# The FFN norms of a two-block network: weight and 1/rms applied behind the transposition of x

## The reference

```python
def rms_norm(x, g):
    y = x * lax.rsqrt(jnp.mean(x * x, axis=-1, keepdims=True) + 1e-6)
    return y * g
def swiglu(x, w_in, w_out):
    a, b = jnp.split(x @ w_in, 2, axis=-1)
    return (jax.nn.silu(a) * b) @ w_out
# block 1
x = x + 0.5 * swiglu(rms_norm(x, ffn1_norm), ffn1_w_in, ffn1_w_out)
u = rms_norm(x, mix_norm) @ w_in      # then RG-LRU, block and memory attention -> mixed
x = x + mixed @ w_out
x = x + 0.5 * swiglu(rms_norm(x, ffn2_norm), ffn2_w_in, ffn2_w_out)
# block 2
for l in range(2):
    h = rms_norm(x, ffn1_norm_pre[l])
    x = x + 0.5 * rms_norm(swiglu(h, ffn1_w_in[l], ffn1_w_out[l]), ffn1_norm_post[l])
    h = rms_norm(x, mix_norm_pre[l])
    x = x + rms_norm(token_mixer(h, mem, ...), mix_norm_post[l])
    h = rms_norm(x, ffn2_norm_pre[l])
    x = x + 0.5 * rms_norm(swiglu(h, ffn2_w_in[l], ffn2_w_out[l]), ffn2_norm_post[l])
```

## Time and profile before

| | us |
|---|---|
| median of 3 runs | 1834.89 (1832.85 to 1840.52) |
| the profiled execution | 1835.6 |
| its span | 1833.6 |
| busy: TensorE | 1795.9 (98%) |
| busy: VectorE | 1059.6 (58%) |
| busy: ScalarE | 910.9 (50%) |
| busy: GpSimd | 45.3 (2%) |

### The profile page before, as it was taken

How to read it: one execution, slowest core, us unless ns; L and a number is a source line. 1 busy time by engine, 2 the same in 40 slices (tenths; PEclk the granted TensorE clock), 3 DMA queues, 4 the chain that set the end, 5 groups by cost and what they waited for, 6 DMA issues and landing times.

```text
span 1833.6 us, 33276 instructions
## 1 busy us (share of the span) xinstructions
PE 1795.9 (98%) x13114; PEld 1658.6 (90%) x13114; DVE 1059.6 (58%) x1393; ACT 910.9 (50%) x1180; POOL 45.3 (2%) x66
## 2 busy tenths in 40 slices
PE   8999998999999999999999999999999999999998
PEld 8999877999999999888899999899999888989997
DVE  5545776554565456565676544554564657675454
ACT  5344565444453445566655344444454566644443
POOL 0000220000000000000000000000000000000000
PEclk9999999999999999999999999999999999999999
DMA  8555423655575555443354554555545442445552
GB/s 313 204 186 202 173 95 113 214 199 185 178 250 185 186 181 207 174 170 116 119 204 168 188 186 176 209 206 190 198 161 211 173 169 94 161 150 207 190 197 94
DMA packets 47857, 329.19 MB, mean 180 GB/s; under 512 B 5393, under 2 KB 5649, under 8 KB 9617
## 3 DMA queue, kind: packets, MB, share of 16 engines
q1 hardware_dynamic: 44496, 316.84, 48.0%
q10 hardware_dynamic: 3264, 11.03, 1.9%
HBM read 326.80 MB, written 1.05 MB: 179 GB/s over the span
## 4 chain that ended last, share of the span: by engine, by line
issue 82%; PE 14%; ACT 2%; POOL 1%; DVE 1%; DMA 0%; DVEq 0%; POOLq 0%; ACTq 0%
PE work L1494 3%; PE work L1493 3%; PE work L1495 3%; PE acc L1493 1%; PE acc L1495 1%; PE acc L1494 1%; POOL rstd L552 1%; ACT prob L720 0%; PE work L1576 0%; PE acc L1586 0%; PE work L1552 0%; DMA const<-const 0%; PE acc L1712 0%; ACT squared L621 0%; ACT hi L609 0%
## 5 line engine op out<-in xcount | busy, mean ns | idle before, releaser
L1003 DVE TENSOR_TENSOR lo<-raw,hi 128x2048 fp32r<-128x2048 f32 x280 | 640.0, 2291 | 468.0 <-ACT hi L601 467.8
L1493 PE MATMUL work<-xT_hi,hi 128*128 128x256 f32 x2752 | 768.4, 279 | 6.9 <-DVE lo L1003 6.4
L1495 PE MATMUL work<-xT_hi,lo 128*128 128x256 f32 x2752 | 763.8, 278 | 0.0
L1494 PE MATMUL work<-xT_lo,hi 128*128 128x256 f32 x2752 | 763.8, 278 | 0.0
L601 ACT ACTIVATE hi<-raw 128x2048 fp32r<-128x2048 f32 x280 | 533.9, 1910 | 236.0 <-PE work L1495 190.3
L1493 PEld LDWEIGHTS work<-xT_hi,hi 128*128 128x128 f32 x2752 | 518.4, 188 | 17.4 <-DVE lo L1003 8.2
L1494 PEld LDWEIGHTS work<-xT_lo,hi 128*128 128x128 f32 x2752 | 518.7, 188 | 2.5
L1495 PEld LDWEIGHTS work<-xT_hi,lo 128*128 128x128 f32 x2752 | 519.4, 189 | 0.0
L1495 PE MATMUL acc<-hi,hT_lo 128*128 128x512 f32 x480 | 189.1, 394 | 0.0
L1494 PE MATMUL acc<-lo,hT_hi 128*128 128x512 f32 x480 | 188.2, 392 | 0.0
L1493 PE MATMUL acc<-hi,hT_hi 128*128 128x512 f32 x480 | 186.9, 389 | 0.0
(11 more groups left out here) (262 smaller groups left out, 1950.7 us busy)
## 6 DMA issues: line engine op xcount, KB each, us to landing
raw<-stream SPq DMA_DIRECT2D x298, 1024.0 KB, 4.8
pre<-pre ACTq DMA_DIRECT2D x7, 512.0 KB, 5.4
mem_in<-mem ACTq DMA_DIRECT2D x3, 1024.0 KB, 7.1
post<-post ACTq DMA_DIRECT2D x6, 512.0 KB, 3.7
x<-x SPq DMA_DIRECT2D x2, 512.0 KB, 4.9
pre<-pre SPq DMA_DIRECT2D x2, 512.0 KB, 3.7
out<-x SPq DMA_DIRECT2D x4, 256.0 KB, 2.0
alibi<-alibi ACTq DMA_DIRECT2D x1, 768.0 KB, 14.8
```

What stands on the lines that cost most here:

```text
L1003: nc.vector.tensor_tensor(lo[:, s, :], raw[:, s, :], hi[:, s, :].bitcast(F32), ALU.subtract).then_inc(lo_ready, 1)
L1493: nc.tensor.matmul(dst, a_hi, b_hi, start=start, stop=False)
L1494: nc.tensor.matmul(dst, a_hi, b_lo, start=False, stop=False)
L1495: return nc.tensor.matmul(dst, a_lo, b_hi, start=False, stop=stop)
```

## The change

- For k = 0 and 3 TensorE transposes x as it is (`x_turned`, 16 transposes of 128 x 128), half by half as x comes, with no sum of squares awaited. The norm's weight is a scale per channel at the evacuation (`x_gain` in `x_high` and `x_low`). Its 24 columns come with the parameters; `pre` and its loads are gone.
- 1/rms comes later. The squares stand behind `x_high`; VectorE spreads 1/rms over a tile (`norm_spread`), TensorE turns it into a row between the first chunk's low products, ScalarE writes it out (`row_out`). A new pass on VectorE, `scaled_a`, multiplies a by it, in every chunk, and the silu works in place on the result. For b the factor is put into the residual: `half_rstd` in block 1; in a layer the post-norm divides it out and only its epsilon is scaled (`norm_eps`).
- `first_chunk` does the high products of the first two units together, except in the first FFN.
- For k = 2 VectorE scales the rows of x by 1/rms (`x_scaled`, 128 x 1024), and 16 transposes follow when both tiles are ready.
- The split of the second unit behind an FFN is taken out of `ffn` and comes behind the norm chain (`B1_MEM + 1`, `L_MEM + 1`), for the second FFNs behind the last post sums.
- Parameters have a semaphore of their own (`params_loaded`), the ring is continuous (`slot`), the loads on SyncE are ordered anew, and the layers are written out in Python on all engines.

The diff, cut to its core and moved left by eight columns ("..." and the hunk lines mark what is left out):

```diff
@@ -491,12 +496,13 @@
...
+def turned_bank(k, r):
+    return acc[:, r, :] if k == 2 else (work[:, 2, :], work[:, 3, :], acc[:, 0, :], acc[:, 1, :])[r]
+def x_gain(sec, k):
+    return (b1p if sec.layer is None else lp)("g_x")[:, KD * (k - k // 2):KD * (k - k // 2) + KD]
@@ -507,32 +513,34 @@
...
+    load(0)
+    sp.dma_start(params[:, KD * 3:B1P_N], b1_params[:, KD * 3:B1P_N]).then_inc(params_loaded, 16)
+    load(1)
+    load(2)
+    at = RING
+    for layer in range(LAYERS):
+        base = B1_UNITS + layer * L_UNITS
+        turns = (base + 1 - at) // RING
+        load_turns(at, at + RING * turns)
+        at += RING * turns
+        sp.dma_start(params[:, 0:LP_N], l_params[layer]).then_inc(params_loaded, 16)
+    turns = (UNITS - at) // RING
+    load_turns(at, at + RING * turns)
+    for n in range(at + RING * turns, UNITS):
+        load(n)
@@ -595,44 +602,48 @@
...
     def x_squares(sec, r, i):
         for c in range(2):
-            act.wait_ge(x_ready, sec.at(12, 12, 4 * r + 2 * i + c + 1))
-            x_half_squares(i, c)
+            if sec.layer is None and r == -1:
+                act.wait_ge(x_loaded[i], 16)
+            else:
+                act.wait_ge(x_ready, sec.at(12, 12, 4 * r + 2 * i + c + 1))
+            nc.scalar.activation(xs[:, i, cols(c)], x[:, i, cols(c)], ACT.Square,
+                                 accum_out=sums[:, 2 * i + c:2 * i + c + 1]).then_inc(sq_ready, 1)
...
     def x_high(sec, k):
...
+        gain = x_gain(sec, k)
+        for r in range(4):
+            act.wait_ge(xT_ready, sec.at(16, 16, 4 * k + r + 1))
+            for c in range(2):
+                kt = 2 * r + c
+                ins = nc.scalar.activation(xT_hi[:, kt, :], turned_bank(k, r)[:, T * c:T * c + T], ACT.Copy,
+                                           scale=gain[:, kt:kt + 1])
+            ins.then_inc(xhi_ready, 1)
+    def row_out(sec, k):
+        act.wait_ge(spread_turned, sec.at(*ROWS, k + 1))
+        nc.scalar.activation(norm_row, work[:, 2, 0:T], ACT.Copy, scale=ROOT_D).then_inc(row_ready, 1)
@@ -647,11 +658,10 @@
...
+        def silu(j):
+            act.wait_ge(scaled_ready, c0 + j + 1)
+            nc.scalar.activation(silu_a, silu_a, ACT.Silu).then_inc(silu_ready, 1)
@@ -661,21 +671,22 @@
...
         split_high(sec, u0 + 2)
-        silu(0, u0)
+        row_out(sec, k)
         split_high(sec, u0 + 3)
+        silu(0)
...
         with act.Fori(1, CHUNKS - 1) as j:
-            silu(j, u0 - 1, j)
             split_high(sec, u0 + 2, j)
+            silu(j)
             split_high(sec, u0 + 3, j)
             high_h(j, u0 + 1, j)
@@ -686,8 +697,6 @@
...
-        if more:
-            split_high(sec, u0 + FFN_UNITS + 1)
@@ -734,22 +743,19 @@
...
     act.wait_ge(half_set, 2)
     nc.scalar.activation(trig[:, 0, 0, :], neg_half[:, 0:ROT], ACT.Square)
+    act.wait_ge(params_loaded, 32)
+    x_high(sec, 0)
+    split_high(sec, B1_FFN1)
+    split_high(sec, B1_FFN1 + 1)
     for i in range(TT):
-        act.wait_ge(x_loaded[i], 16)
-        for c in range(2):
-            x_half_squares(i, c)
-    split_high(sec, B1_FFN1)
-    x_high(sec, 0)
-    split_high(sec, B1_FFN1 + 1)
-    load_pre(sec, 1)
+        x_squares(sec, -1, i)
@@ -759,10 +765,10 @@
     ffn(sec, B1_FFN1, 0, lambda: mem_squares(sec), b1p("g_mem"))
     for i in range(TT):
         x_squares(sec, 0, i)
+    split_high(sec, B1_MEM + 1)
     split_high(sec, B1_MEM + 2)
+    x_high(sec, 2)
     split_high(sec, B1_MEM + 3)
-    x_high(sec, 2)
@@ -830,36 +836,34 @@
...
-    split_high(sec, B1_OUT + 4)
+    split_high(sec, B1_FFN2)
+    split_high(sec, B1_FFN2 + 1)
+    x_high(sec, 3)
     for i in range(TT):
         x_squares(sec, 1, i)
-    x_high(sec, 3)
-    split_high(sec, B1_FFN2 + 1)
...
+    ffn(sec, B1_FFN2, 1, angles)
+    split_high(sec, B1_UNITS + 1)
...
+    for layer in range(LAYERS):
         sec = Section(layer)
...
+        act.wait_ge(params_loaded, 16 * (3 + layer))
+        x_high(sec, 0)
+        load_post(sec, 0)
         for i in range(TT):
             x_squares(sec, -1, i)
-        split_high(sec, L_FFN1)
-        x_high(sec, 0)
...
             post_sums(sec, 0, L_MEM - 1, i)
             x_squares(sec, 0, i)
+        split_high(sec, L_MEM + 1)
@@ -984,13 +987,16 @@
             split_high(sec, L_OUT + w + 2)
         for i in range(TT):
             post_sums(sec, 1, L_FFN2 - 1, i)
+        split_high(sec, L_FFN2 + 1)
+        x_high(sec, 3)
+        load_post(sec, 2)
+        for i in range(TT):
             x_squares(sec, 1, i)
-        load_post(sec, 2)
-        x_high(sec, 3)
-        split_high(sec, L_FFN2 + 1)
-        ffn(sec, L_FFN2, 1, more=False)
+        ffn(sec, L_FFN2, 1, more=layer + 1 < LAYERS)
         for i in range(TT):
             post_sums(sec, 2, L_UNITS - 1, i)
+        if layer + 1 < LAYERS:
+            split_high(sec, L_UNITS + 1)
@@ -1013,39 +1019,42 @@
...
+    def x_scaled(sec, p, i):
+        dve.wait_ge(x_ready, sec.at(12, 12, 2 * i + 2))
+        dve.wait_ge(sq_ready, sec.at(14, 14, 6 + 2 * i + 2))
+        ask_root(i, sums[:, 2 * i:2 * i + 2], D * EPS)
         root_ready(sec, p)
-        nc.vector.tensor_scalar(diag[:, i, :], ident, rstd[:, i:i + 1], ROOT_D, ALU.mult, ALU.mult).then_inc(xs_ready, 1)
+        nc.vector.tensor_scalar(xs[:, i, :], x[:, i, :], rstd[:, i:i + 1], ROOT_D, ALU.mult, ALU.mult).then_inc(xs_ready, 1)
+    def norm_spread(sec, k, p):
+        dve.wait_ge(sq_ready, sec.at(14, 14, (4, 14)[k]))
+        parts = sums[:, 0:2 * TT].rearrange("p (i c) -> p i c", c=2)
+        nc.vector.scalar_tensor_tensor(var[:, 0:TT], parts[:, :, 0], D * EPS, parts[:, :, 1], ALU.add, ALU.add).then_inc(pow_asked, 1)
+        root_ready(sec, p)
+        nc.vector.tensor_copy(spread, rstd[:, 0:TT].unsqueeze(2).to_broadcast([P, TT, P])).then_inc(spread_ready, 1)
+        if sec.layer is None:
+            return step.mark(nc.vector.tensor_scalar(half_rstd, rstd[:, 0:TT], 0.5 * ROOT_D, None, ALU.mult))
+        return step.mark(nc.vector.tensor_scalar(norm_eps, var[:, 0:TT], EPS, None, ALU.mult))
     def x_low(sec, k):
...
+        for r in range(4):
+            dve.wait_ge(xhi_ready, sec.at(16, 16, 4 * k + r + 1))
+            for c in range(2):
+                kt = 2 * r + c
+                ins = nc.vector.scalar_tensor_tensor(xT_lo[:, kt, :], turned_bank(k, r)[:, T * c:T * c + T], gain[:, kt:kt + 1],
+                                                     xT_hi[:, kt, :].bitcast(F32), ALU.mult, ALU.subtract)
+            ins.then_inc(xlo_ready, 1)
     def mem_scaled(sec, p):
@@ -1066,6 +1075,13 @@
...
+        def scaled_a(j, n, trip=0):
+            dve.wait_ge(unit_used, sec.unit(n + 1) + trip * RING)
+            wait(dve, h_ready, c0 + j)
+            nc.vector.tensor_tensor(silu_a.rearrange("p (c t) -> p c t", c=2), work[:, 0, :].rearrange("p (c t) -> p c t", c=2),
+                                    norm_row.unsqueeze(1).to_broadcast([P, 2, T]), ALU.mult).then_inc(scaled_ready, 1)
         def gated(j, n, trip=0):
@@ -1079,6 +1095,8 @@
...
         split_low(sec, u0 + 2)
+        dve.wait_ge(row_ready, sec.at(*ROWS, k + 1))
+        scaled_a(0, u0)
         split_low(sec, u0 + 3)
@@ -1086,12 +1104,14 @@
...
         with dve.Fori(1, CHUNKS - 1) as j:
+            scaled_a(j, u0 - 1, j)
@@ -1103,23 +1123,21 @@
...
-            nc.vector.scalar_tensor_tensor(x[:, i, cols(c)], acc[:, 2 * i + c, :], scale, x[:, i, cols(c)], ALU.mult,
+            nc.vector.scalar_tensor_tensor(x[:, i, cols(c)], acc[:, 2 * i + c, :], scale or half_rstd[:, i:i + 1], x[:, i, cols(c)], ALU.mult,
                                            ALU.add).then_inc(x_ready, 1)
...
         for c in range(2):
             dve.wait_ge(ysq_ready, sec.at(0, 12, 4 * r + 2 * i + c + 1))
             if c == 1:
-                ask_root(2 + i, ysums[:, 2 * i:2 * i + 2])
+                ask_root(2 + i, ysums[:, 2 * i:2 * i + 2], eps)
@@ -1161,16 +1179,14 @@
...
-    dve.sem_inc(lo_ready, 1)
-    dve.wait_ge(ident_loaded, 16)
-    for i in range(TT):
-        x_scaled(sec, 0, i, i)
+    dve.wait_ge(params_loaded, 32)
     x_low(sec, 0)
     split_low(sec, B1_FFN1)
     split_low(sec, B1_FFN1 + 1)
+    step.after(norm_spread(sec, 0, 0))
@@ -1178,11 +1194,12 @@
...
+        residual(sec, 0, B1_MEM - 1, i, None)
+        x_scaled(sec, 2 + i, i)
+    split_low(sec, B1_MEM + 1)
     split_low(sec, B1_MEM + 2)
+    x_low(sec, 2)
     split_low(sec, B1_MEM + 3)
-    x_low(sec, 2)
@@ -1284,12 +1301,12 @@
...
+    split_low(sec, B1_FFN2)
     for i in range(TT):
         residual(sec, 1, B1_FFN2 - 1, i, 1.0)
-        x_scaled(sec, 3, 8 + i, i)
     x_low(sec, 3)
     split_low(sec, B1_FFN2 + 1)
+    step.after(norm_spread(sec, 1, 7))
@@ -1309,29 +1326,25 @@
...
+    for layer in range(LAYERS):
...
+        dve.wait_ge(params_loaded, 16 * (3 + layer))
         x_low(sec, 0)
-        split_low(sec, L_FFN1)
         split_low(sec, L_FFN1 + 1)
...
+        step.after(norm_spread(sec, 0, 0))
```

(60 more changed lines are left out.)

286 lines of the change are left out of this document (93 added, 193 removed).

## The result

The changed kernel takes 1847.94 us (median of 6 runs, 1847.03 to 1848.42), the kernel before 1833.21 us beside it (6 runs). The ratio is 1.0062, with a 95% interval of 1.0039 to 1.0085: slower by 0.6%, where 1817.8 us and a gain were forecast. The profiled execution has a span of 1846.3 us, 12.7 more than before.

What follows compares the result with a forecast made beforehand. TensorE was taken as busy nearly the whole span. Entries 23.8 plus block 1's mix norm 3.3, less layers' mix norms 7.6 and start 2.4, give 17.1 us off: median 1834.89 to 1817.8, range 1806 to 1827.

Steps and rivals of the forecast that it cites:

- What stays: Inside an FFN: a chunk stays 16 us of TensorE without a gap; the added VectorE pass and moved silu cost nothing.
- signs that the prediction gave for being wrong: No mix-norm wait, TensorE waiting for `silu_a` or `scaled_a`, or engine pauses in the straight code where the loop was.
- Rival C: Chunk loop: `scaled_a` holds bank 0 so TensorE stands 0.4 us in each of 66 chunks; 1844 us, chance 0.03.
- entry of layer 0: First FFN of layer 0: fillers, fp32 passes and waiting go, first chunk ends at 509.3 instead of 514.4; gain 5.1 us.
- entry of layer 1: First FFN of layer 1: no back-edge pause, first chunk ends at 1174.5 instead of 1183.5; gain 9.0 us, the largest term.
- block 1 mix norm: Mix norm in block 1: squares start earlier because the second unit's split moves behind the norm; gain 3.3 us.
- entry of block 1's FFN2: Second FFN of block 1: first chunk ends at 323.6 instead of 326.4; gain 2.8 us.
- layers' mix norm: Mix norm in each layer: the late split of `L_MEM + 1` stalls TensorE 4.3 us and lowers its clock; loss 3.8 us.
- entries of the layers' FFN2: Second FFN in each layer: first chunk ends at 985.2 instead of 988.65; gain 3.4 us, twice.
- start: Kernel start: evacuating x waits for all parameters, then the first split; first product at 16.0; loss 2.4 us (0 to 4).
- Rival B: FFN entries: the norm row comes late (6 us) or the clock drops (3 to 6 us); about 1823 us, chance 0.25.
- Layers written out: Layer loops as straight code: waits lose register arithmetic, taken as nothing; bounded by 2.4 us gain or loss a layer.

Runs made afterwards that it cites:

- good layout: The changed kernel with 160 unused bytes a partition behind the parameters: 1813.9 us, ratio 0.9873 to the kernel before.
- the run with the other start: The good layout with the first unit split before x is evacuated, fillers mostly behind the transposes, and alibi and mem_in loaded later: 1807.3 us.

## Why the prediction was wrong, point by point

**The step that failed** is the first sentence of "What stays": that a chunk keeps its time because its instructions and waits stay. The step of a TensorE product depends on where the buffers lie, and the change moved them by 96 bytes and by 4000: the in step went from 113.6 to 116.7 ns and the chunk from 16.40 to 16.80 us. Against the good layout the span is 31.8 us longer (1846.3 and 1814.5), 22.8 of it in the bodies and the rest nearly all in the stages between. No rival named it, and of the signs that the prediction gave for being wrong none came: they are waits and pauses, and this loss shows in neither. The length of a chunk was misread besides: the earlier trace rows show a window of 16 us that 119 products touch, and the chunk lasts 16.40. Rival C had the right price, 0.4 us a chunk and 1844, for a mechanism that is not there: no wait for `scaled_a`, and the pass done twice costs nothing. It would have been right for a wrong reason.

On the good layout (`room(160)`), whose steps and chunks are those of the kernel before, the span is 19.0 us shorter; 17.1 were forecast. By its terms:

| term | forecast | measured on the good layout |
|---|---|---|
| entry of layer 0 | 5.1 | 4.7 |
| entry of layer 1 | 9.0 | 8.6, of it 3.3 by the layers written out alone |
| block 1 mix norm | 3.3 | 3.5 (10.86 to 7.39) |
| entry of block 1's FFN2 | 2.8 | 2.9 (the rest of that stage's 6.4) |
| layers' mix norm | -3.8 each | -2.9 each (15.06 to 17.95) |
| entries of the layers' FFN2, and all else in their mix stages | 3.4 each | 5.5 and 3.9 |
| start | -2.4 | -4.6 |

The sum is nearer than its terms: misses of about 2 us, the start one way and the layers' stages the other, cancel in part. That is luck.

**The entries** were read well. In the changed kernel's timeline of layer 0's entry, whose last product starts at 502.33, against the earlier trace rows:

```profile
502.56 0.60 PE L1614 MATMUL work<-const,x 128*128 128x128 f32 x4
...
503.91 0.84 ACT L639 ACTIVATE xT_hi<-work,params 128x256 fp32r<-128x256 f32 x2 [2.03 <-PE work L1614]
...
504.89 0.47 PE L1560 MATMUL work<-xT_hi,hi 128*128 128x256 f32 x2 [0.42 <-ACT xT_hi L639]
```

Products start 2.3 us after the end of the last one; 2.2 were forecast, 0.4 of it a wait for pair 0. **Rival B's clock drop** did not come: the granted clock of the stretch with the transposes and of the one behind it is 1.00.

```profile
502.50:504.90 2.40, 1.98 (x18) 1.71 (x16) 0.80 (x2) 0.99 (x3) 0.00 (x0) 1.00 0.73 299
504.90:508.00 3.10, 3.10 (x26) 3.10 (x27) 3.10 (x9) 3.10 (x10) 0.00 (x0) 1.00 0.50 169
```

It was 1.00 at the entries of block 1's FFN2 and of the layers' FFN2, too. The Trainium skill, "TensorE: Matmul & The Clock Gate", Part 4: PE-mode transpose, says that transpose mode does not count as being busy for the clock. The prediction took drops as likely by that; with 1.98 us of transposes in these 2.40 us none came, and these runs do not test a longer stretch of them.

**The mix norm** had the right mechanism. The stall was 3.0 us (4.3 forecast), the clock fell as said, and the edit that puts the split early takes both away. The price of a drop was right, too: 1.6 us forecast, and 1.6 to 1.7 between the layer norms of the good layout with one drop (17.9, 18.0 us) and the one without in the run with the other start (16.3). What the prediction did not have is that the drop can stay away.

**The start** had the right order and one thing missed: the fillers. They stood in TensorE's queue ahead of the transposes and held them, although x had landed at 6.3 us and the parameters at 10.8 (11.0 forecast). Until 10.3 us they start 0.21 us apart and from then on 0.11. The clock column reads 1.00 for both stretches, so that the first one ran at the lower level is inferred from the spacing alone.

```profile
5.19 6.25 PE L1605 MATMUL work<-const 128*128 128x128 f32 x32 [5.19 <-DMA const<-const]
...
11.27 0.60 PE L1614 MATMUL work<-const,x 128*128 128x128 f32 x4
...
17.51 1.86 PE L1560 MATMUL work<-xT_hi,hi 128*128 128x256 f32 x7 [4.33 <-ACT hi L608]
```

The first product came at 17.5, not 16.0, and 26 products took the next 4.5 us at a granted clock of 0.67, where I had put 1.6 us for the clock in all. In the good layout's run the clock there was 0.50 for 5.9 us, from the first product on.

```profile
17.50:22.00 4.50, 4.49 (x26) 4.49 (x27) 4.50 (x3) 4.50 (x10) 0.00 (x0) 0.67 0.52 182
```

**Layers written out** I costed at nothing beyond the back edge, between a gain and a loss of 2.4 a layer; in the kernel before, written out alone, 1.7 a layer were gained in the mix stages.

## What to carry to other kernels

A change that adds a column to a buffer moves all buffers behind it, and the step of a kernel bound by TensorE can depend on that, as it did here: before any other reason is looked for, compare the step from product to product in a loop that the change did not touch, and the addresses of the operands. Busy shares, waits and the granted clock stay silent on it. When it has moved, try the eight 32-byte offsets within 256 bytes before judging the change; here 63 us lie between the best and the worst of them (1813.9 and 1876.7), three times what the change itself brings. And a stage that the edit did not touch, but that came out 2 to 5 us shorter in one profile, is no gain until more executions show it; the granted clock behind its waits tells.
